# Moving the high halves of the weights by 32 bytes within each partition

## What is computed

```
px = hx @ w_in[i]                       # 1024 -> 6144 columns
attn_x = diff_attention(q_x, keys, vals, lam, attn_norm_g[i], lam_init)
y_x = merge_branches(conv_x, attn_x, g_x, ...)
x = x + gx1 * y_x
x = x + gx2 * sqrelu_mlp(modulate(rmsnorm(x, norm2_g[i]), sx2, ax2), w_mlp1[i], w_mlp2[i])
```

## Time and profile before

| | |
|---|---|
| median of two runs | 2087.31 us |
| span of the profiled execution | 2089.1 us |
| TensorE matmuls busy | 2024.6 us, 97% |
| TensorE weight loads busy | 1789.9 us, 86% |
| VectorE busy | 1363.7 us, 65% |
| ScalarE busy | 1019.1 us, 49% |
| GpSimd busy | 162.3 us, 8% |
| DMA | 294.56 MB, mean 141 GB/s |

### The profile page before, as it was taken

How to read it: one execution, slowest core, us unless ns; L and a number is a source line. 1 busy time by engine, 2 the same in 40 slices (tenths; PEclk the granted TensorE clock), 3 DMA queues, 4 the chain that set the end, 5 groups by cost and what they waited for, 6 DMA issues and landing times.

```text
span 2089.1 us, 36236 instructions
## 1 busy us (share of the span) xinstructions
PE 2024.6 (97%) x13946; PEld 1789.9 (86%) x13946; DVE 1363.7 (65%) x2114; ACT 1019.1 (49%) x2014; POOL 162.3 (8%) x174
## 2 busy tenths in 40 slices
PE   6999999999999999999999999999999999999998
PEld 5899657888788888879967999999998989888897
DVE  5699688344565564577977667776766555886455
ACT  5475575324422322358457454445824444675443
POOL 0000000000000001000000002223120111000110
PEclk9999999999999999999999999999999999999999
DMA  7322374222222222233255545554302555443553
GB/s 287 122 82 102 122 283 161 81 101 101 81 83 98 100 100 83 98 108 135 83 203 217 179 147 181 185 192 176 115 21 82 181 181 188 184 164 137 191 183 121
DMA packets 40896, 294.56 MB, mean 141 GB/s; under 512 B 4544, under 2 KB 4544, under 8 KB 5456
## 3 DMA queue, kind: packets, MB, share of 16 engines
q1 hardware_dynamic: 40464, 290.73, 38.4%
q0 software_dynamic: 320, 2.26, 0.3%
HBM read 291.93 MB, written 1.05 MB: 140 GB/s over the span
## 4 chain that ended last, share of the span: by engine, by line
PE 88%; DVE 5%; ACT 4%; issue 1%; DMA 1%; SPq 0%; DVEq 0%; ACTq 0%
PE psum L652 21%; PE psum L654 21%; PE psum L653 20%; PE psum L1017 3%; PE psum L1021 3%; PE psum L1018 3%; PE psum L890 2%; PE psum L1224 2%; DVE weights_lo L1964 2%; PE psum L793 2%; PE psum L912 1%; PE psum L692 1%; PE psum L693 1%; PE psum L694 1%; ACT weights_hi L1363 1%
## 5 line engine op out<-in xcount | busy, mean ns | idle before, releaser
L1964 DVE TENSOR_TENSOR weights_lo<-raw_weights,weights_hi 128x2048 fp32r<-128x2048 f32 x225 | 512.6, 2291 | 163.1 <-ACT weights_hi L1363 162.7
L1363 ACT ACTIVATE weights_hi<-raw_weights 128x2048 fp32r<-128x2048 f32 x225 | 429.0, 1910 | 152.6 <-DMA raw_weights<-in_weights 133.1
L2043 DVE SCALAR_TENSOR_TENSOR xT<-psum,mods,xT 128x256 f32<-128x256 f32 x408 | 181.0, 479 | 199.9 <-PE psum L654 196.5
L652 PE MATMUL psum<-h_hi,weights_hi 128*128 128x512 f32 (+1 forms) x832 | 279.9, 336 | 0.1
L654 PE MATMUL psum<-h_lo,weights_hi 128*128 128x512 f32 (+1 forms) x832 | 279.8, 336 | 0.0
L653 PE MATMUL psum<-h_hi,weights_lo 128*128 128x512 f32 (+1 forms) x832 | 278.1, 334 | 0.0
L2840 POOL TENSOR_TENSOR ffsq<-ff 128x256 f32<-128x256 f32 (+1 forms) x128 | 118.2, 925 | 1592.1 <-ACT ff L1450 1107.6
L652 PE MATMUL psum<-weights_hi,h_hi 128*128 128x256 f32 x704 | 197.5, 280 | 0.0
L653 PE MATMUL psum<-weights_lo,h_hi 128*128 128x256 f32 x704 | 195.5, 278 | 0.0
L654 PE MATMUL psum<-weights_hi,h_lo 128*128 128x256 f32 x704 | 195.5, 278 | 0.0
L652 PE MATMUL psum<-g_hi,weights_hi 128*128 128x256 f32 x688 | 193.7, 282 | 0.0
(11 more groups left out here) (423 smaller groups left out, 4277.6 us busy)
## 6 DMA issues: line engine op xcount, KB each, us to landing
raw_weights<-in_weights SPq DMA_DIRECT2D x273, 1024.0 KB, 4.8
staged_x<-in_x_rows SPq DMA_DIRECT2D x1, 2048.0 KB, 10.0
masks<-in_masks POOLq DMA_DIRECT2D x1, 1152.0 KB, 6.8
ln_rows<-in_ln_rows POOLq DMA_DIRECT2D x1, 1024.0 KB, 6.8
out<-outrow SPq DMA_DIRECT2D x4, 256.0 KB, 2.1
rows<-in_rows SPq DMA_DIRECT2D x1, 584.0 KB, 9.7
consts<-in_consts SPq DMA_DIRECT2D x1, 388.0 KB, 3.8
cols<-in_cols SPq DMA_DIRECT2D x1, 306.0 KB, 2.8
```

What stands on the lines that cost most here:

```text
L652: mm(out, *pair(wh, vh), start=i == 0, stop=False)
L1363: f(w_hi[:, s, :], raw[:, s, :], ACT.Copy).then_inc(hi_done, 1)
L1964: tt_(w_lo[:, s, :], raw[:, s, :], w_hi[:, s, :].bitcast(F32), ALU.subtract).then_inc(lo_done, 1)
L2043: last = stt(xT[:, m, c], b[:, c], mods[:, l, which + m, v:v + 1], xT[:, m, c], ALU.mult, ALU.add)
```

## The change

Between `weights_lo` and `weights_hi` a tile of 8 float32 in each partition is added, which nothing reads or writes:

```diff
--- before
+++ after
@@ -247,6 +247,7 @@
         raw = sb("raw_weights", [P, RAW, CHUNK])
 
         w_lo = nc.alloc_sbuf_tensor_at("weights_lo", [P, RAW, CHUNK], F32R, offset=ring_at)
+        sb("pad", [P, 8])
         w_hi = sb("weights_hi", [P, RAW, CHUNK], F32R)
         xT = sb("xT", [P, KT, SEQ + CTX])
         cols = sb("cols", [P, COLS_N])
```

## The result

The change made the kernel slower. Before: 2087.31 us (2 runs, 2086.70 to 2087.92). After: 2108.18 us (2 runs, 2106.60 to 2109.76). The ratio is 1.0093, with a 95% interval of 1.0068 to 1.0118. It is less than the 2% named as the limit of a measurement, yet well clear of no change. The profiled execution took 2109.76 us, its span 2108.0; before, the span was 2089.1.

What follows compares the result with a forecast made beforehand. TensorE's stream of weight products was taken to set the time, matmuls being busy 97% of the span. All terms were 0, so the 2089.1 us span, less 1.8 us for the runs' median, gave 2087 us, range 2072 to 2108.

Steps and rivals of the forecast that it cites:

- TensorE's reads of `weights_hi`, 7,200 matmuls: Weight products reading the moved tile: taken at 0 because L705 and L912 agree; bounds plus or minus 31 us.
- Addresses repeat there, so they alone do not choose the pace: TensorE's 256-column products: two paces 4.3 ns apart on the same ring slots and activations, perhaps from restarts after a pause.
- slower rival: TensorE products on the moved tile: mid-block starts need a further 64-byte block, 4.3 ns each, 31 us, 2118; chance 0.13.
- fewer than 220 matmuls from 600 us: 512-column stretch, 600 to 650 us: a count below 220 would show TensorE slower on the moved tile.
- not for L653: TensorE's weight products: slowing would appear in all forms with `weights_hi` but spare L653.
- faster rival: TensorE's streamed operand and overlapping weight load stop conflicting once 32 bytes apart: 23 us gained, 2064; chance 0.08.
- 427 rising towards 443: 256-column stretch, 1250 to 1300 us: the matmul count would rise this way if TensorE became faster.
- VectorE's split: Reads `raw_weights` and `weights_hi` 225 times at 2291 ns: cost 0, upper bound +10 us.
- ScalarE's: Split writing `weights_hi` 225 times at 1911 ns: cost 0; 5% longer would add 1 us.
- the small tiles: `xT`, `cols`, `cond`, `rows`, `consts` and `root` trade kinds of offset: sum 0.
- DMA: Ring and weight transfers stay put; `cols`, `consts` and `rows` come once beside work: cost 0.
- the weaker half of the slower case: TensorE slower by half a step on each matmul reading the moved tile: 15 us, held within the range.

Runs made afterwards that it cites:

- a4_all32: Kernel before with both weight halves, the small tiles and the arena of activations all moved by 32 bytes, distances kept: 2090.23 us, ratio 1.0004.
- h_rel192: Kernel before with `ssq` placed ahead of the weights ring, bringing the arena-to-weights distance from 64 to 192: 2090.53 us, ratio 1.0003.
- a3_small_only: Kernel before with the 32-byte pad behind `weights_hi`, so only the small tiles move as in the change: 2089.79 us, ratio 1.0007.
- a5_weights32: Kernel before with both weight halves moved by 32 bytes and the arena left, distance 32 for both: 2106.76 us, ratio 1.0092.
- e_weights16: Kernel before with all weights shifted by 16 bytes inside larger tiles, distance 48: 2105.17 us, ratio 1.0086.
- e_weights8: Kernel before with all weights shifted by 8 bytes inside larger tiles, distance 56: 2103.64 us, ratio 1.0075.
- b2_arena32: Kernel before with the arena of activations alone moved by 32 bytes, distance 96 for both weight halves: 2115.69 us, ratio 1.0132.
- h_rel128: Kernel before with `rows` and `ssq` placed ahead of the weights ring, distance 128: 2112.00 us, ratio 1.0107.
- d1_rel0: Kernel before with `rows` and `small` placed ahead of the weights ring, distance 0: 2097.43 us, ratio 1.0045.
- g2_mixed192: Kernel before with the activations of certain 512-column stages moved by 192 bytes, distance 0 there, 64 elsewhere: 2081.81 us, ratio 0.9961.
- b1_lo32: Kernel before with `raw_weights` and `weights_lo` moved to distance 32; `weights_hi` landed at distance 0 instead of the intended 64: 2106.67 us, ratio 1.0077.
- d2_rel256: Kernel before with `rows` alone placed ahead of the weights ring, 256 bytes from the ring's place in d1_rel0: 2097.60 us, ratio 1.0045.
- g_mixed: Kernel before with the activations of certain 512-column stages moved by 64 bytes, distance 128 there: 2093.67 us, ratio 1.0022.

## Why the prediction was wrong, point by point

**The step that failed** is "TensorE's reads of `weights_hi`, 7,200 matmuls", which I took at 0. The row was read rightly and was the wrong one: in L705 both operands lie in `consts`, and in L912 both lie on multiples of 64. In the built program the distance between the two operands is 0 modulo 256 in both lines, before the change and after it. The pair compares two *places*, and a4_all32 confirms that places cost nothing (1.0004). It never compared two *distances*, and the change alters distances. The nearest row was near in the one respect that does not matter. The term is -1.5 to +8.4 us by kind of product, +17.8 in sum.

**"Addresses repeat there, so they alone do not choose the pace"** was half of an insight. Two paces at one set of addresses showed that something else chooses; after a pause the stream falls into the one or the other. The trace of before has 73 stretches of 24 or more products of 256 columns without a pause; 22 run at 113.3 to 114.2 ns, 51 at about 117.8, none in between, and none changes its pace inside. After the change none of the 73 has a mean below 117. So part of the loss is that a fast pace, into which the stream often fell, is no longer there. The addresses say which paces there are to choose from: 113.3 and 117.8 ns at distance 64, one pace of 119.9 at distance 0. From the two paces I drew that addresses were harmless.

**The slower rival** had the right engine, the right sign and about the right size, and the wrong mechanism. It named a block of 64 bytes that begins in the middle; a4_all32 puts every operand there for nothing. It gave 2118, with 4.3 ns on each of 7,200 products. Measured are +3.1 ns on average where weights are streamed with 256 columns, +3.2 where activations are streamed with 512, but +0.7 for the most frequent kind, activations with 256, and -1.5 ns in the last. Its sign to look for, fewer than 220 matmuls from 600 us, came true (217). Its other sign, "not for L653", holds for streamed weights of 256 columns (278 ns before and after) and fails elsewhere: with 512 columns of activations the product of L653 lost most, 227.3 to 232.7 ns.

**The faster rival** had the idea that the runs bear out, that the streamed operand and the weight load have to do with each other by their addresses, and the wrong sign for this shift. I wrote against it that the weight load is busy all the time at either pace, which said nothing about distance. 64 is not the worst distance but a fair one. Its mark, "427 rising towards 443", appeared in h_rel192 (444), and paid for it elsewhere.

**The terms at 0 that held:** VectorE's split (median 2291 ns, both times), ScalarE's (1911 and 1910), the small tiles (a3_small_only, 1.0007), and DMA (the waits behind it 133.1 and 133.4 us). The bounds of +10 and +1 us around the splits were not needed, and the row named for the first, `zc` with `root`, kept its 548 ns.

**The range** ended at 2108, and the result is 2108.18; that it came so near the edge is chance. The text reckons the weaker half of the slower case at 15 us, half a step on 7,200 products, which is 2102; no sum leads to the 6 us above that. The profile shows 17.8. The text did say that a pace depending on "where its operand begins" was something "which no row of a rounded-float32 matmul here can exclude". The rows allowed more weight on it. But the dependence that came out, on the distance between two operands, appears in it only as the mechanism of the faster rival. The Trainium skill, page SBUF — State Buffer, section Specifications (TRN2), has lines of 16 bytes, by which a shift of whole lines takes no more of them. The forecast of 0 agreed with that; the runs do not: shifting the weights by 16 and 32 bytes costs 0.86% and 0.92%. The same page, section Who interferes with whom, has PE wait on no one. For other engines nothing here speaks against that, but the distance between TensorE's own two operands does set its pace, by up to 1.3% of this kernel.

## What the runs showed of the hardware

Not expected at all: the pace of a matmul in rounded float32 depends on the signed distance between its two operands, and everything seen here fits a period of 256 bytes. Nanoseconds for three products, start to start in the trace, at full clock without pauses:

| distance | kernel | act. 256 | weights 256 | act. 512 | weights 512 | ratio |
|---|---|---|---|---|---|---|
| 64 | before | 352.7 | 343.9 | 686.8 | 699.9 | 1 |
| 64 | a4_all32 | 352.2 | 344.7 | 686.8 | 699.9 | 1.0004 |
| 32 and 64 | after | 354.7 | 353.6 | 696.7 | 695.3 | 1.0093 |
| 32 | a5_weights32 | 350.1 | 354.9 | 700.0 | 699.8 | 1.0092 |
| 48 | e_weights16 | 350.1 | 357.2 | 698.4 | 702.5 | 1.0086 |
| 56 | e_weights8 | 352.3 | 360.4 | 692.2 | 697.5 | 1.0075 |
| 96 | b2_arena32 | 359.8 | 353.4 | 700.1 | 701.2 | 1.0132 |
| 128 | h_rel128 | 356.1 | 356.0 | 697.4 | 696.4 | 1.0107 |
| 192 | h_rel192 | 343.0 | 352.8 | 700.0 | 686.9 | 1.0003 |
| 0 | d1_rel0 | 359.9 | 359.8 | 680.6 | 683.2 | 1.0045 |
| 0 and 64 at 512, 64 at 256 | g2_mixed192 | 352.5 | 342.6 | 683.1 | 687.1 | 0.9961 |

(The columns say what is streamed, activations or weights, and how many columns. The values are three times the mean of one product. In g2_mixed192 about six tenths of the products that stream 512 columns of activations and eight tenths of those that stream 512 of weights stand at 0, the others at 64.) At 0 and at 128 both kinds of stream agree to 3 ns, as they must if turning the sign round exchanges them, and at 64 and 192 they are exchanged. At 512 columns distance 0 is the best of the table; at 256 columns it is the worst in sum.

Three things stay open. No run tells whether a product's stream meets its own stationary operand or the one that is loaded for the next. After the change the interval of 512 columns in which the moved tile is only loaded lost 5 ns and the one in which it is only held 1.5, which leans to the loaded one; in b1_lo32 both such intervals are slow. The period of 256 rests on d1_rel0 against d2_rel256, on g_mixed against g2_mixed192, and on 0 differing from 128; a distance of 160 or 224 was not tried. And what in the memory has this period is not shown by anything here. What chooses between the two paces after a pause was not tried either; it may be why the kernel before had medians from 2087.3 to 2090.7 us in five jobs.

## What to carry to other kernels

An edit that only moves a tile need not be free if TensorE reads it: note the start of the streamed and of the stationary operand in each large product, and compare the distance between them modulo 256 bytes before and after, not the alignment of either. Read the addresses from the built program: 16 bytes asked for can take 32. When you look for a row that bounds a new placement, ask which relation the change alters, and whether the two rows that you compare differ in that relation. A difference of under 3% in the pace of matmuls with no wait and no other engine behind it is worth a sweep of placements; here 192 bytes in some stages gave 0.4% for nothing.
